# Second matrix of the MLP in seven block products instead of eight, with weight sums made by accumulating DMA

## The chip, the core and the metric

The kernel runs on one core of one Trainium2 chip. The metric is the device time of one execution in microseconds (us); the time before is the median of three runs. Four engines matter here: TensorE (PE in the profile; its weight loads are PEld), VectorE (DVE), ScalarE (ACT) and GpSimd (POOL). SyncE (SP) only issues DMAs.

## What is computed

One decoder layer on 512 tokens of width 1024, float32 throughout. A token mixer with three branches comes first (some 640 us of the time) and is not touched by the change. The part that is changed is the MLP behind it:

```python
h = rms_norm(x, norm_ffn_pre[l])
f = jnp.square(jax.nn.relu(h @ w_ff1[l])) @ w_ff2[l]
x = x + rms_norm(f, norm_ffn_post[l])
```

`w_ff1` is 1024 x 4096 and `w_ff2` is 4096 x 1024.

## The kernel before

Every float32 matrix product is made of three products in a rounded format: each operand is split into a high part (ScalarE copies it into the format, `copy_hi`) and a low part (VectorE subtracts the high part from the original, `lo`), and `products` (L936 to L938) issues high by high, high by low and low by high, in this order, into the same bank of PSUM. A matmul has a stationary operand of 128x128 and moves 512 columns.

Weights come as 176 "units" of 128x1024 (512 KB), in the order in which they are used. SyncE loads unit u into one of two raw slots (`raw`, L268) as soon as the low part of the unit before last in it is made. ScalarE copies it to `w_hi` (L375) when TensorE has finished unit u-4, because `w_hi` and `w_lo` are rings of four; VectorE makes `w_lo` (L603) behind it. TensorE waits for `w_lo_ready`, does the unit and counts up `unit_done`. So behind each finished unit ScalarE and VectorE prepare the unit four places on, and each engine works in the order of its program.

The hidden layer is worked in four quarters of 1024 channels. For each quarter there are eight "up" units (`up`, `channel_unit`: the weights are stationary, the 512 tokens move, eight steps of K, 24 matmuls, result in bank n of the eight banks) and eight "down" units (`token_unit`: 128 tokens by 128 hidden channels are stationary, 512 columns of weights move, four token chunks by two steps of K by three, 24 matmuls). The first three up units of a quarter are written ahead of the loop's end, which changes the program text but not the order.

Behind each up unit (`hidden_unit`) ScalarE makes relu from PSUM into one half of `duo` (L574) and its square into `a_hi` (L576), then splits the weights; VectorE splits the weights, squares in float32 (L885) and subtracts `a_hi` (L603). A down unit n below four waits for `hidden_lo` of the two tiles that it reads. After the fourth and the eighth down unit VectorE adds four banks into `by_token` in SBUF (L900). The last quarter is summed another way: its second half of weights is kept in `c_hi` and `c_lo`, and `resident_products` finishes one block of 128 tokens by 512 columns after another, so that the end of the kernel can overlap it.

GpSimd does little in this stage. It clears `by_token` (L367, 3.5 us, before the first quarter) and makes the inverse roots at the end.

Of the kernel before, what the change touches and what calls it, by code (L numbers as in the profile page):

```python
# [65 lines left out]
U_FF = U_OUT + KT  # L66
PER_QUARTER = 2 * KT
UNITS = U_FF + QUARTERS * PER_QUARTER

# [46 lines left out]
def build(nc, x_d, units_d, cols_d, rows_d, ws_d, bs_d, out_d):  # L116
    with ExitStack() as ctx:
        def sb(name, shape, dt=F32):
            return ctx.enter_context(nc.sbuf_tensor(name, shape, dt))

        def sem(name):
# [5 lines left out]
        w_lo = sb("w_lo", [P, RING, D], F32R)  # L127

        a_hi = sb("a_hi", [P, KT, SEQ], F32R)
        a_lo = sb("a_lo", [P, KT, SEQ], F32R)  # L130

        b_hi = sb("b_hi", [P, KT, SEQ], F32R)
        b_lo = sb("b_lo", [P, KT, SEQ], F32R)

# [22 lines left out]
        ws_lo = sb("ws_lo", [P, P], F32R)  # L157
        bs_row = sb("bs_row", [P, 2, P])
        duo = sb("duo", [P, 2, SEQ])
        th, h_copy = duo[:, 0, :], duo[:, 1, :]  # L160
        prod = sb("prod", [P, CONV_A - 1 + SEQ])
        y_a = sb("y_a", [P, SEQ])
# [14 lines left out]
        ps = ctx.enter_context(nc.psum_tensor("ps", [P, 8, 512], F32))  # L177


        raw_loaded = [sem(f"raw_loaded{n}") for n in range(RAW)]  # L180
        x_loaded = [sem(f"x_loaded{n}") for n in range(CH)]
# [65 lines left out]
        hidden_sq = sem("hidden_sq")  # L247
        hidden_lo = sem("hidden_lo")
        mlp_sum = sem("mlp_sum")
        out_weighted = sem("out_weighted")  # L250
# [14 lines left out]
        @block.sync  # L265
        def _(sp):
            def load(unit, slot):
                sp.dma_start(raw[:, slot, :], units_d[unit]).then_inc(raw_loaded[slot], 16)  # L268

            for c in range(CH):  # L270
                sp.dma_start(resid[:, c, :], x_d[c * P:(c + 1) * P, :]).then_inc(x_loaded[c], 16)
                if c < RAW:
                    load(c, c)
            sp.dma_start(cols[:, :, :], cols_d).then_inc(cols_loaded, 16)
            with sp.Fori(1, UNITS // RAW) as i:
                for slot in range(RAW):
                    sp.wait_ge(w_lo_ready, i * RAW + (slot - RAW + 1))
                    load(i * RAW + slot, slot)
            for c in range(CH):
# [8 lines left out]
        def _(pool):  # L288
# [77 lines left out]
            pool.wait_ge(turned, 4 * CH)  # L366
            nc.gpsimd.memset(wide[:, :], 0.0).then_inc(wide_cleared, 1)  # L367
            for c in range(CH):
                inverse_rms(3 * CH + c, 4 * CH + 2 * c, halves=True)
# [3 lines left out]
        def _(act):  # L373
# [3 lines left out]
            def split_hi(u, into=None, free=True):  # L377

                act.wait_ge(raw_loaded[u.raw], u.loads())
                if free and u.first >= RING:  # L380
                    act.wait_ge(unit_done, u.times(1, 1 - RING))
                copy_hi(w_hi[:, u.ring, :] if into is None else into,
                        raw[:, u.raw, :]).then_inc(w_hi_ready, 1)

            def after(u):
# [159 lines left out]
            def first_ff(units):  # L545
                for n in units:
                    act.wait_ge(unit_done, U_OUT + n + 1)
                    split_hi(Count(U_FF + n), free=False)

# [17 lines left out]

            def hidden_unit(u, n):

                after(u)  # L570
                if n.first % KT >= 2:
                    act.wait_ge(hidden_lo, n.times(1, -1))
                h = duo[:, n.first % 2, :]
                nc.scalar.activation(h, ps[:, n.first % KT, :], ACT.Relu).then_inc(hidden_relu, 1)  # L574
                act.wait_ge(hidden_relu, n.times(1, 1))
                nc.scalar.activation(a_hi[:, n.first % KT, :], h, ACT.Square).then_inc(hidden_hi, 1)  # L576
                split_hi(u.plus(RING))

            with act.Fori(0, QUARTERS - 1) as q:
                for n in range(KT):  # L580
                    hidden_unit(Count(U_FF + n, q, PER_QUARTER), Count(n, q, KT))
                for n in range(KT):
                    u = Count(U_FF + KT + n, q, PER_QUARTER)
                    after(u)
                    split_hi(u.plus(RING))
            for n in range(KT):
                hidden_unit(Count(U_FF + (QUARTERS - 1) * PER_QUARTER + n), Count((QUARTERS - 1) * KT + n))

            for n in range(CH):
                split_hi(Count(UNITS - CH + n), resident(c_hi, n), free=False)  # L590

            for c in range(CH):
                for half in range(2):
                    act.wait_ge(mlp_sum, ((QUARTERS - 1) * CH + c) * 2 + half + 1)
                    sum_squares(4 * CH + 2 * c + half, by_token[:, c, half * HALF:(half + 1) * HALF],
                                ps[:, 2 * c + half, :])
# [3 lines left out]
        def _(dve):  # L600
# [6 lines left out]
            def split_lo(u, into=None, hi=None):  # L607

                dve.wait_ge(w_hi_ready, u.times(1, 1))
                lo(w_lo[:, u.ring, :] if into is None else into, raw[:, u.raw, :],  # L610
                   w_hi[:, u.ring, :] if hi is None else hi).then_inc(w_lo_ready, 1)

            def after(u):
# [234 lines left out]
            for c in range(CH):  # L848
# [18 lines left out]
                if c == CH - 1:  # L867
                    split_lo(Count(U_FF + 2))
                dve.wait_ge(rstd_ready, CH + 2 * c + 2)
# [4 lines left out]
                for n in {CH - 2: (0, 1), CH - 1: (3,)}.get(c, ()):  # L874
                    split_lo(Count(U_FF + n))
            turned_lo(2 * CH - 1, CH - 1, b_hi, b_lo, 2 * (CH - 1))

            def hidden_unit(u, n):

                place = n.first % KT  # L880
                h = duo[:, n.first % 2, :]
                after(u)
                split_lo(u.plus(RING))
                dve.wait_ge(hidden_hi, n.times(1, 1))
                nc.vector.tensor_tensor(h, h, h, ALU.mult).then_inc(hidden_sq, 1)  # L885
                dve.wait_ge(hidden_sq, n.times(1, 1))
                lo(a_lo[:, place, :], h, a_hi[:, place, :]).then_inc(hidden_lo, 1)

            dve.wait_ge(wide_cleared, 1)
            with dve.Fori(0, QUARTERS - 1) as q:  # L890
                for n in range(KT):
                    hidden_unit(Count(U_FF + n, q, PER_QUARTER), Count(n, q, KT))
                for n in range(KT):
                    u = Count(U_FF + KT + n, q, PER_QUARTER)
                    after(u)
                    if n % CH == CH - 1:
                        half = n // CH
                        for c in range(CH):
                            y = by_token[:, c, half * HALF:(half + 1) * HALF]
                            nc.vector.tensor_tensor(y, y, ps[:, half * CH + c, :],  # L900
                                                    ALU.add).then_inc(mlp_sum, 1)
                    split_lo(u.plus(RING))
            for n in range(KT):
                hidden_unit(Count(U_FF + (QUARTERS - 1) * PER_QUARTER + n), Count((QUARTERS - 1) * KT + n))
            for n in range(CH):
                split_lo(Count(UNITS - CH + n), resident(c_lo, n), resident(c_hi, n))


            sums = (QUARTERS - 1) * 2 * CH
            dve.wait_ge(mlp_sum, sums)  # L910
# [22 lines left out]
        def _(pe):  # L933
# [173 lines left out]

            with pe.Fori(0, QUARTERS - 1) as q:
                for n in range(EARLY, KT):
                    up(Count(U_FF + n, q, PER_QUARTER), n)  # L1110
                for n in range(KT):
                    if n < CH:
                        pe.wait_ge(hidden_lo, Count(0, q, KT).times(1, 2 * n + 2))
                    token_unit(Count(U_FF + KT + n, q, PER_QUARTER), n % CH, n // CH, a_hi, a_lo)
                for n in range(EARLY):
                    up(Count(U_FF + PER_QUARTER + n, q, PER_QUARTER), n)
            for n in range(EARLY, KT):
                up(Count(U_FF + (QUARTERS - 1) * PER_QUARTER + n), n)
            before = (QUARTERS - 1) * KT
            resident_products(UNITS - KT, a_hi, a_lo, c_hi, c_lo,  # L1120
                              lambda piece: pe.wait_ge(hidden_lo, before + 2 * piece + 2),
                              lambda n, piece: None)
# [55 lines left out]
```

## Time and profile before

| | us |
|---|---|
| median of three runs (1006.65 to 1007.42) | 1007.12 |
| span of the profiled execution, first to last instruction | 1005.2 |
| what lies outside the span (median less span) | 1.9 |
| TensorE busy in the span | 986.9 |
| VectorE busy | 619.2 |
| ScalarE busy | 335.2 |
| GpSimd busy | 68.3 |

The median is that of timed runs; the profiled execution is known by its span. Busy times are read with care. A matmul's row gives the time from its start to its modelled end, and matmuls overlap, so what one matmul costs is the distance between two starts and not the length of a row. A timeline row gives the start in us from the span's start, the length in us, the engine, the line, the operation and the shapes, and in square brackets how long the engine sat idle before it and what released it. Rows with a count (x4) are several instructions merged. In the rows by stretch each engine's busy us stands with its number of instructions, then the granted clock of TensorE as a part of full speed, the mean busy share of the sixteen DMA engines (0.29 is 29%), and what they moved in GB/s.

### The profile page before, as it was taken

The page shows a single profiled execution, that of the slowest core. Times are in us where ns is not written, and L with a number is a line of the kernel's source. Part 1 is how long each engine was busy: PE and PEld are TensorE (multiplying, and loading weights), DVE is VectorE, ACT ScalarE, POOL GpSimd, SP SyncE. Part 2 cuts the span into 40 slices and gives each one's busy share as a digit, 9 for nine tenths or more (in the row PEclk, how much of TensorE's full clock was granted, in tenths as well). Part 3 has the DMA queues.
Part 4 walks back from the last instruction along what each step waited for, and adds up shares of the span by engine and source line. Part 5 has one row for each costly group of instructions (what it writes and reads, how often), then busy time and mean ns, then how long its engine had stood idle before and what let it go on. Part 6 is the DMA issues. An engine that isn't in the chain of part 4 may idle for free.

```text
span 1005.2 us, 12693 instructions
## 1 busy us (share of the span) xinstructions
PE 986.9 (98%) x4476; PEld 821.5 (82%) x4476; DVE 619.2 (62%) x765; ACT 335.2 (33%) x453; POOL 68.3 (7%) x83
## 2 busy tenths in 40 slices
PE   5999999999999999999999999999999999999997
PEld 4888888888888888888888888898888888888886
DVE  5348888888988988876674344844344334433545
ACT  5333332333233222224463232543224214313331
POOL 3000000000000011114000000210000000000001
PEclk9999999999999999999999999999999999999999
DMA  6323223233222222233245323132322323322222
GB/s 218 118 78 125 91 89 94 99 97 101 89 92 95 72 96 83 96 117 105 98 135 204 104 84 105 57 110 89 102 91 97 104 83 104 104 86 103 88 80 84
DMA packets 28861, 102.27 MB, mean 102 GB/s; under 512 B 3360, under 2 KB 3488, under 8 KB 28832
## 3 DMA queue, kind: packets, MB, share of 16 engines
q1 hardware_dynamic: 27216, 96.64, 28.6%
q10 hardware_dynamic: 1104, 4.19, 1.2%
q0 software_dynamic: 512, 1.05, 0.5%
q8 instruction: 18, 0.29, 0.1%
q14 instruction: 11, 0.09, 0.0%
HBM read 99.77 MB, written 2.10 MB: 101 GB/s over the span
## 4 chain that ended last, share of the span: by engine, by line
PE 98%; DMA 1%; DVE 1%; POOL 0%; ACT 0%; issue 0%; DVEq 0%; POOLq 0%; ACTq 0%
PE ps L936 31%; PE ps L937 31%; PE ps L938 31%; PE ps L1091 1%; PE ps L1090 1%; PE ps L1089 1%; PE ps L976 1%; DMA conf<-x_in 1%; PE ps L1039 0%; PE ps L1040 0%; PE ps L1038 0%; ACT ps L389 0%; DVE wide L628 0%; POOL rstd L310 0%; POOL meansq L306 0%; DVE a_lo L603 0%
## 5 line engine op out<-in xcount | busy, mean ns | idle before, releaser
L603 DVE TENSOR_TENSOR w_lo<-raw,w_hi 128x1024 fp32r<-128x1024 f32 x168 | 207.2, 1234 | 257.6 <-ACT w_hi L375 257.1
L375 ACT ACTIVATE w_hi<-raw 128x1024 fp32r<-128x1024 f32 x168 | 177.1, 1055 | 286.3 <-PE ps L938 217.6
L936 PE MATMUL ps<-a_hi,w_hi 128*128 128x512 f32 x576 | 225.4, 391 | 0.0
L937 PE MATMUL ps<-a_lo,w_hi 128*128 128x512 f32 x576 | 224.2, 389 | 0.0
L938 PE MATMUL ps<-a_hi,w_lo 128*128 128x512 f32 x576 | 224.1, 389 | 0.0
L674 DVE SCALAR_TENSOR_TENSOR conf<-glu,cols,conf (+1 forms) x240 | 186.8, 778 | 27.5 <-DVE conf L674 26.4
L936 PE MATMUL ps<-b_hi,w_hi 128*128 128x512 f32 x360 | 140.2, 390 | 0.0
L938 PE MATMUL ps<-b_hi,w_lo 128*128 128x512 f32 x360 | 140.1, 389 | 0.0
L937 PE MATMUL ps<-b_lo,w_hi 128*128 128x512 f32 x360 | 140.0, 389 | 0.0
L936 PEld LDWEIGHTS ps<-a_hi,w_hi 128*128 128x128 f32 x576 | 108.2, 188 | 22.7 <-DVE w_lo L603 0.2
L937 PEld LDWEIGHTS ps<-a_lo,w_hi 128*128 128x128 f32 x576 | 108.2, 188 | 22.6 <-issue 0.5
L938 PEld LDWEIGHTS ps<-a_hi,w_lo 128*128 128x128 f32 x576 | 108.1, 188 | 22.6
L936 PE MATMUL ps<-w_hi,a_hi 128*128 128x512 f32 x288 | 112.9, 392 | 1.5 <-DVE a_lo L603 1.4
L938 PE MATMUL ps<-w_hi,a_lo 128*128 128x512 f32 x288 | 112.5, 391 | 0.0
L937 PE MATMUL ps<-w_lo,a_hi 128*128 128x512 f32 x288 | 112.5, 391 | 0.0
L936 PEld LDWEIGHTS ps<-b_hi,w_hi 128*128 128x128 f32 x360 | 67.6, 188 | 14.3 <-DVE b_lo L604 0.3
L938 PEld LDWEIGHTS ps<-b_hi,w_lo 128*128 128x128 f32 x360 | 67.6, 188 | 14.1
L937 PEld LDWEIGHTS ps<-b_lo,w_hi 128*128 128x128 f32 x360 | 67.6, 188 | 13.9
L936 PEld LDWEIGHTS ps<-w_hi,a_hi 128*128 128x128 f32 x288 | 54.3, 189 | 13.3 <-DVE a_lo L603 2.2
L938 PEld LDWEIGHTS ps<-w_hi,a_lo 128*128 128x128 f32 x288 | 54.3, 189 | 11.5
L937 PEld LDWEIGHTS ps<-w_lo,a_hi 128*128 128x128 f32 x288 | 54.4, 189 | 11.1
L574 ACT ACTIVATE duo<-ps 128x512 f32<-128x512 f32 x32 | 19.1, 598 | 103.5 <-PE ps L938 96.4
(140 smaller groups left out, 891.7 us busy)
## 6 DMA issues: line engine op xcount, KB each, us to landing
raw<-units_in SPq DMA_DIRECT2D x176, 512.0 KB, 3.3
glu<-rows_in ACTq DMA_DIRECT2D x4, 512.0 KB, 10.9
conf<-x_in SPq DMA_DIRECT2D x4, 512.0 KB, 8.0
conf<-x_in ACTq DMA_DIRECT2D x1, 2048.0 KB, 9.2
y_out<-wide SPq DMA_DIRECT2D x8, 256.0 KB, 2.1
ws_raw<-ws_in POOLq DMA_DIRECT2D x8, 64.0 KB, 2.1
bs_row<-bs_in POOLq DMA_DIRECT2D x8, 64.0 KB, 3.1
cols<-cols_in SPq DMA_DIRECT2D x1, 156.0 KB, 9.2
```

The costliest lines, as they stand in the source:

```text
L375: return nc.scalar.activation(dst, src, ACT.Copy, scale=scale)
L574: nc.scalar.activation(h, ps[:, n.first % KT, :], ACT.Relu).then_inc(hidden_relu, 1)
L603: return nc.vector.tensor_tensor(dst, src, hi, ALU.subtract)
L674: nc.vector.scalar_tensor_tensor(out=conf[:, tile, :], in0=glu[:, tile, k:k + SEQ], scalar=cols[:, tile, COL_CONF + k:COL_CONF + k + 1], i ...
L936: nc.tensor.matmul(ps[:, bank, :], left_hi, right_hi, start=first, stop=False)
L937: nc.tensor.matmul(ps[:, bank, :], left_hi, right_lo, start=False, stop=False)
L938: return nc.tensor.matmul(ps[:, bank, :], left_lo, right_hi, start=False, stop=final)
L976: mm = nc.tensor.transpose(ps[:, banks + g, k * P:(k + 1) * P], by_token[:, c, at:at + P], ident[:, :])
L1089: nc.tensor.matmul(out, w_hi[:, u.ring, w], b_hi[:, k, tokens], start=k == 0, stop=False)
L1090: nc.tensor.matmul(out, w_hi[:, u.ring, w], b_lo[:, k, tokens], start=False, stop=False)
L1091: mm = nc.tensor.matmul(out, w_lo[:, u.ring, w], b_hi[:, k, tokens], start=False, stop=k == KT - 1)
```

## The change

The down products of the first three quarters are done in another way; the last quarter stays as it is. For one quarter the product is 512 tokens by 1024 hidden channels by 1024 columns. It is cut in halves along all three sides, and the eight half-size products are replaced by seven (Strassen's scheme, in a form with differences and sums). The steps are these:

- TensorE: the eight down units of 24 matmuls are replaced by 14 "pieces" (seven products in two halves of K each) of 12 matmuls, each with 128x128 stationary and 512 columns moving. The up units are the same, with the tiles of the hidden layer in the order 0, 4, 1, 5, 2, 6, 3, 7. The loop over quarters is written out.
- Left operands: seven blocks of 128x256 for each pair of hidden tiles instead of four. `hidden_pair`: ScalarE does relu of both tiles, each followed by the split of the weights four units on; one square of 128x1024 in place; a copy of two blocks into `set_hi`. VectorE makes five differences (`combo`, three instructions) and the low part of the two blocks. ScalarE copies the five differences into `set_hi`, and VectorE makes their low part. The square in float32 of VectorE (L885) goes.
- Right operands: five of the seven products need the sum or difference of two weight blocks. SyncE loads the first block; GpSimd issues a DMA with `accum_op=add` that adds the second block from memory to the one in the raw slot. For product 1 ScalarE first negates the block in the slot.
- Results: each product is added to or subtracted from one or two quarters of `by_token`, 24 instructions of 128x512 on VectorE for each quarter of the hidden layer instead of 8.
- Raw slots: eight instead of two, six of them laid over buffers that are no longer in use at this stage. `a_hi` and what follows it in SBUF are reused for `set_hi`, `set_lo` and two of the slots.

```diff
+PRODUCTS = {
+    3: (0, (0, 1), (1, 1), 2, ((0, 1, 1), (1, 1, 1))),
+    6: (2, (0, 0), (0, 1), 4, ((1, 1, 1),)),
...
+PIECES = ((3, 0), (6, 0), (3, 1), (6, 1), (4, 0), (2, 0), (4, 1), (2, 1),
+          (1, 0), (5, 0), (1, 1), (5, 1), (7, 0), (7, 1))
...
+NEGATED_AFTER = {0: 8, 2: 10}
...
+            for u in range(U_FF, UNITS):
+                slot = FF_SLOT[u]
+                if earlier_in_slot(u):
+                    sp.wait_ge(w_lo_ready, earlier_in_slot(u)[-1] + 1)
...
+                elif slot < 6:
+                    sp.wait_ge(unit_done, U_FF)
+                else:
+                    sp.wait_ge(mixed_in, 4 * CH)
+                sp.dma_start(slots[slot], units_d[source(u)]).then_inc(raw_loaded[slot], 16)
...
+                    if product == 1:
+                        negated += 1
+                        pool.wait_ge(raw_negated, negated)
+                    else:
+                        pool.wait_ge(raw_loaded[slot], ff_loads(u))
+                    pool.dma_start(slots[slot], units_d[source(u, second=True)],
+                                   accum_op=ALU.add).then_inc(raw_added[slot], 16)
...
+            def hidden_pair(q, p):
+
+                n = q * CH + p
+                for e in range(2):
+                    u = ff_unit(q, 2 * p + e)
+                    act.wait_ge(unit_done, u + 1)
+                    if n:
+                        act.wait_ge(set_lo_ready, 2 * n - 1)
+                    nc.scalar.activation(duo[:, e, :], ps[:, 2 * p + e, :], ACT.Relu).then_inc(hidden_relu, 1)
+                    ff_hi(u + RING)
+                act.wait_ge(hidden_relu, 2 * n + 2)
+                nc.scalar.activation(duo[:, :, :], duo[:, :, :], ACT.Square).then_inc(pair_squared, 1)
+                act.wait_ge(pair_squared, n + 1)
+                copy_hi(set_hi[:, 0:2, p, :], pair[:, 0:4:3, :]).then_inc(set_hi_ready, 1)
+                act.wait_ge(combo_ready, 3 * n + 3)
+                copy_hi(set_hi[:, 2:SETS, p, :], combo[:, :, :]).then_inc(set_hi_ready, 1)
...
+                for n in range(len(PIECES)):
+                    act.wait_ge(unit_done, piece_unit(q, n) + 1)
+                    ff_hi(piece_unit(q, n) + RING)
+                    if n in NEGATED_AFTER:
+                        u = piece_unit(q, NEGATED_AFTER[n])
+                        act.wait_ge(raw_loaded[FF_SLOT[u]], ff_loads(u))
+                        copy_hi(slots[FF_SLOT[u]], slots[FF_SLOT[u]], -1.0).then_inc(raw_negated, 1)
...
+                for e in range(2):
+                    u = ff_unit(q, 2 * p + e)
+                    dve.wait_ge(unit_done, u + 1)
+                    ff_lo(u + RING)
+                dve.wait_ge(pair_squared, n + 1)
...
+                nc.vector.tensor_tensor(combo[:, 0:2, :], pair[:, 1:4:2, :], pair[:, 0:4:2, :],
+                                        ALU.subtract).then_inc(combo_ready, 1)
+                nc.vector.tensor_tensor(combo[:, 2:4, :], pair[:, 2:4, :], pair[:, 0:2, :],
+                                        ALU.subtract).then_inc(combo_ready, 1)
+                nc.vector.tensor_tensor(combo[:, 4, :], pair[:, 0, :], pair[:, 3, :],
+                                        ALU.subtract).then_inc(combo_ready, 1)
+                dve.wait_ge(set_hi_ready, 2 * n + 1)
+                lo(set_lo[:, 0:2, p, :], pair[:, 0:4:3, :], set_hi[:, 0:2, p, :]).then_inc(set_lo_ready, 1)
+                dve.wait_ge(set_hi_ready, 2 * n + 2)
+                lo(set_lo[:, 2:SETS, p, :], combo[:, :, :], set_hi[:, 2:SETS, p, :]).then_inc(set_lo_ready, 1)
...
+                for n, (product, h) in enumerate(PIECES):
+                    dve.wait_ge(unit_done, piece_unit(q, n) + 1)
+                    ff_lo(piece_unit(q, n) + RING)
...
+                    for t in range(2):
+                        for m_half, n_half, sign in into:
+                            y = by_token[:, 2 * m_half + t, n_half * HALF:(n_half + 1) * HALF]
+                            nc.vector.tensor_tensor(y, y, ps[:, bank + t, :],
+                                                    ALU.add if sign > 0 else ALU.subtract).then_inc(mlp_sum, 1)
...
+            def piece(q, n):
...
+                ready(Count(u))
+                pe.wait_ge(set_lo_ready, 2 * (q * CH + 2 * h + 2))
+                if h == 0 and product in (3, 6, 4, 2):
+                    pe.wait_ge(hidden_relu, q * KT + bank + 2)
+                elif h == 0:
+                    pe.wait_ge(mlp_sum, sums_before(q, piece_done({1: 3, 5: 6, 7: 4}[product])))
+                for t in range(2):
+                    for k in range(2):
+                        at, w = slice(t * P, (t + 1) * P), slice(k * HALF, (k + 1) * HALF)
+                        mm = products(bank + t, set_hi[:, which, 2 * h + k, at], set_lo[:, which, 2 * h + k, at],
+                                      w_hi[:, u % RING, w], w_lo[:, u % RING, w],
+                                      (h, k) == (0, 0), (h, k) == (1, 1))
+                mm.then_inc(unit_done, 1)
```

An up unit of the next quarter also waits (`bank_summed`) until VectorE has emptied its bank.

## Rows read from the trace of the kernel before

**Rows 1.** The head and part 1 of the page.

```profile
span 1005.2 us, 12693 instructions
PE 986.9 (98%) x4476; PEld 821.5 (82%) x4476; DVE 619.2 (62%) x765; ACT 335.2 (33%) x453; POOL 68.3 (7%) x83
```

**Rows 2.** The page's part 4, the chain that ended last, by engine.

```profile
PE 98%; DMA 1%; DVE 1%; POOL 0%; ACT 0%; issue 0%; DVEq 0%; POOLq 0%; ACTq 0%
```

**Rows 3.** Busy time by stretch: us, engines, granted clock, DMA share, GB/s.

```profile
525.00:535.00 10.00, 10.00 (x46) 8.29 (x45) 4.34 (x5) 3.09 (x5) 0.00 (x0) 1.00 1.02 399
750.00:810.00 60.00, 60.00 (x266) 49.70 (x265) 25.29 (x30) 19.17 (x24) 0.00 (x0) 1.00 0.29 96
998.70:1005.20 6.50, 0.07 (x1) 0.00 (x0) 2.79 (x4) 0.72 (x2) 0.86 (x2) 0.82 0.21 81
```

**Rows 4.** Timeline (start, us, engine, line), TensorE, sixty matmuls of a down product.

```profile
789.62 0.39 PE L938 MATMUL ps<-w_hi,a_lo 128*128 128x512 f32 x1
...
803.00 0.39 PE L937 MATMUL ps<-w_lo,a_hi 128*128 128x512 f32 x1
```

**Rows 5.** Group by line and shape: busy us, mean ns, idle before.

```profile
L603 DVE TENSOR_TENSOR a_lo<-duo,a_hi 128x512 fp32r<-128x512 f32 x32 | 22.2, 692 | 1.1
```

**Rows 6.** Timeline, ScalarE, one hidden unit, and two weight copies back to back.

```profile
775.77 0.60 ACT L574 ACTIVATE duo<-ps 128x512 f32<-128x512 f32 x1 [3.23 <-PE ps L938]
776.40 0.63 ACT L576 ACTIVATE a_hi<-duo 128x512 fp32r<-128x512 f32 x1
776.94 1.04 ACT L375 ACTIVATE w_hi<-raw 128x1024 fp32r<-128x1024 f32 x1
...
956.46 1.04 ACT L375 ACTIVATE w_hi<-raw 128x1024 fp32r<-128x1024 f32 x1
957.40 1.04 ACT L375 ACTIVATE c_hi<-raw 128x1024 fp32r<-128x1024 f32 x1
```

**Rows 7.** Timeline, VectorE, one hidden unit, and the sums of one half.

```profile
778.01 1.22 DVE L603 TENSOR_TENSOR w_lo<-raw,w_hi 128x1024 fp32r<-128x1024 f32 x1 [2.89 <-ACT w_hi L375]
779.16 0.68 DVE L885 TENSOR_TENSOR duo<-duo 128x512 f32<-128x512 f32 x1
...
911.77 2.48 DVE L900 TENSOR_TENSOR wide<-wide,ps 128x512 f32<-128x512 f32 x4 [2.99 <-PE ps L938]
914.17 1.22 DVE L603 TENSOR_TENSOR w_lo<-raw,w_hi 128x1024 fp32r<-128x1024 f32 x1
```

**Rows 8.** Timeline, start of the kernel: TensorE resumes after a wait.

```profile
12.56 0.69 DVE L603 TENSOR_TENSOR a_lo<-ps,a_hi 128x512 fp32r<-128x512 f32 x1 [0.16 <-ACT a_hi L375]
...
13.30 0.29 PEld L936 LDWEIGHTS ps<-w_hi,a_hi 128*128 128x128 f32 x1 [1.81 <-DVE a_lo L603]
13.30 0.80 PE L936 MATMUL ps<-w_hi,a_hi 128*128 128x512 f32 x1 [1.41 <-DVE a_lo L603]
```

**Rows 9.** Timeline, TensorE, spacing early in the kernel and somewhat later.

```profile
13.89 0.63 PE L937 MATMUL ps<-w_lo,a_hi 128*128 128x512 f32 x1
...
14.32 0.63 PE L938 MATMUL ps<-w_hi,a_lo 128*128 128x512 f32 x1
...
19.16 0.40 PE L937 MATMUL ps<-w_lo,a_hi 128*128 128x512 f32 x1
19.39 0.39 PE L938 MATMUL ps<-w_hi,a_lo 128*128 128x512 f32 x1
```

**Rows 10.** The page's parts 3 and 6: DMA queues; issues with KB and us to landing.

```profile
q1 hardware_dynamic: 27216, 96.64, 28.6%
q0 software_dynamic: 512, 1.05, 0.5%
...
raw<-units_in SPq DMA_DIRECT2D x176, 512.0 KB, 3.3
ws_raw<-ws_in POOLq DMA_DIRECT2D x8, 64.0 KB, 2.1
```

**Rows 11.** Groups by line: what an issue costs GpSimd.

```profile
L318 POOL DMA_DIRECT2D ws_raw<-ws_in x8 | 4.7, 587 | 174.8 <-DVE y_s L757 174.8
```

More of the change, by code:

```diff
@@ L177, in build @@
         ps = ctx.enter_context(nc.psum_tensor("ps", [P, 8, 512], F32))
[L180 removed]
+        set_hi = over("set_hi", [P, SETS, CH, SEQ // 2], "a_hi", dt=F32R)
+        set_lo = over("set_lo", [P, SETS, CH, SEQ // 2], "a_hi", SETS * 2 * SEQ, dt=F32R)
+        raw_c = over("raw_c", [P, 2, D], "a_hi", SETS * 4 * SEQ)
+        raw_v = over("raw_v", [P, 2, D], "v_hi")
+        combo = over("combo", [P, SETS - 2, SEQ // 2], "y_a")
+        pair = duo[:, :, :].rearrange("p j (h t) -> p (j h) t", h=2)
+        slots = [raw[:, 0, :], raw[:, 1, :], raw_v[:, 0, :], raw_v[:, 1, :],
+                 raw_c[:, 0, :], raw_c[:, 1, :], row[0], row[1]]
+        raw_loaded = [sem(f"raw_loaded{n}") for n in range(SLOTS)]
+        raw_added = [sem(f"raw_added{n}") for n in range(SLOTS)]
+        raw_negated = sem("raw_negated")
         x_loaded = [sem(f"x_loaded{n}") for n in range(CH)]
@@ L383, in split_hi, with ff_hi @@
                         raw[:, u.raw, :]).then_inc(w_hi_ready, 1)
+            def ff_hi(u, into=None, free=True):
+                slot = FF_SLOT[u]
+                if has_second(u):
+                    act.wait_ge(raw_added[slot], seconds(u))
+                else:
+                    act.wait_ge(raw_loaded[slot], ff_loads(u))
+                if free:
+                    act.wait_ge(unit_done, u + 1 - RING)
+                copy_hi(w_hi[:, u % RING, :] if into is None else into, slots[slot]).then_inc(w_hi_ready, 1)
             def after(u):
@@ L874, in _ @@
                 for n in {CH - 2: (0, 1), CH - 1: (3,)}.get(c, ()):
-                    split_lo(Count(U_FF + n))
+                    ff_lo(U_FF + n)
             turned_lo(2 * CH - 1, CH - 1, b_hi, b_lo, 2 * (CH - 1))
[L878 to L884, printed above, removed]
-                nc.vector.tensor_tensor(h, h, h, ALU.mult).then_inc(hidden_sq, 1)
-                dve.wait_ge(hidden_sq, n.times(1, 1))
-                lo(a_lo[:, place, :], h, a_hi[:, place, :]).then_inc(hidden_lo, 1)
@@ L889, in _ @@
[L889 to L902, printed above, removed]
@@ L1117, in _, with bank_summed @@
-            for n in range(EARLY, KT):
-                up(Count(U_FF + (QUARTERS - 1) * PER_QUARTER + n), n)
-            before = (QUARTERS - 1) * KT
+            def bank_summed(q, n):
+                for product in {0: (2,), 2: (1,), 4: (5,), 6: (7,)}.get(n, ()):
+                    pe.wait_ge(mlp_sum, sums_before(q, piece_done(product)))
+            def piece(q, n):
+                product, h = PIECES[n]
+                which, _, _, bank, _ = PRODUCTS[product]
+                u = piece_unit(q, n)
+                ready(Count(u))
[11 more added lines that the diff above has]
+                mm.then_inc(unit_done, 1)
@@ L1120, in _ @@
+            for q in range(STRASSEN):
+                for n in range(EARLY if q == 0 else 0, KT):
+                    if q:
+                        bank_summed(q - 1, n)
+                    up(Count(ff_unit(q, n)), n)
+                for n in range(len(PIECES)):
+                    piece(q, n)
+            for n in range(KT):
+                bank_summed(STRASSEN - 1, n)
+                up(Count(U_LAST + n), n)
             resident_products(UNITS - KT, a_hi, a_lo, c_hi, c_lo,
-                              lambda piece: pe.wait_ge(hidden_lo, before + 2 * piece + 2),
+                              lambda piece: pe.wait_ge(hidden_lo, 2 * piece + 2),
```

148 lines of the change are left out of this document (107 added, 41 removed), and 5 rows, old and new, of the table PRODUCTS.

## Prediction

> **What bounds the kernel now.** I read the head of the page first, then the chain that ended last, then the stretches, then single rows. TensorE is busy for 986.9 of 1005.2 us [rows 1], and the chain is 98% TensorE [rows 2]. Busy time alone can deceive, since matmuls overlap, so the spacing decides: sixty matmuls in a row start between 789.62 and 803.00, 59 distances in 13.38 us, 0.2268 us each, over two unit boundaries and without a gap [rows 4]. One unit of 24 matmuls is 5.44 us, as the ScalarE rows also say: they come back every 5.44 us. In the MLP the clock is full, the DMA engines are 29% busy, VectorE works 25 of 60 us and ScalarE 19 [rows 3]. So in this stage only two things move the time: fewer matmuls, and gaps in TensorE's stream.
>
> **What the change removes.** Down products of one quarter: 8 x 24 = 192 matmuls become 14 x 12 = 168, all with 512 moving columns. Three quarters: 72 fewer, 72 x 0.2268 = 16.3 us. Nothing hides under it: it is the bounding engine.
>
> **What it adds ahead of the first late pieces.** This is the one place where I find a new wait. Before, the last hidden tiles of a quarter were needed only by the fourth down unit, 3 x 5.44 us later. Now the third piece (product 3, second half of K) waits for all of pair 3, and TensorE has only two pieces, 24 matmuls, 5.44 us, to do in between. The chain behind the quarter's eighth up unit, from the start of its relu (0):
>
> ScalarE. Relu 0.60 long; the next independent instruction can start 0.09 before a row's end (776.40 + 0.63 against 776.94), so the weight split starts at 0.51 and ends at 1.55. Two 1024-wide instructions follow at 0.94 [rows 6], so the square of 128x1024, priced like that split, runs 1.45 to 2.49. A dependent instruction starts 0.03 after the end (776.37 to 776.40): copy of two blocks, 512 wide, 2.52 to 3.15.
>
> VectorE. It starts 0.03 after ScalarE ends (777.98 to 778.01) and next starts 1.15 later [rows 7]: its weight split runs 1.58 to 2.81. Then the differences, at the 0.69 of a 512-wide subtraction [rows 5], 0.60 apart as the four sums are (2.40 us, [rows 7]): 2.73, 3.33, and the 256-wide one from 3.93. Its length by the slope between 512 and 1024 columns (1.22 less 0.69 for 512) is 0.42, so it ends at 4.35. The two blocks' low part goes 4.28 to 4.97.
>
> Then ScalarE copies five differences, 1280 wide: 1.04 plus half of the step from 512 to 1024 (1.04 less 0.63), 1.25, from 4.38 to 5.63. VectorE takes their low part, 1.22 plus 0.27, 1.49, from 5.66 to 7.15. TensorE resumes 0.05 after such a release (13.25 to 13.30, [rows 8]), and perhaps after one weight load of 0.2 more: 7.20 to 7.40.
>
> TensorE is free at 5.47 (the relu starts 0.20 after the last matmul's start, so the next starts at 0.03, and 24 x 0.2268 = 5.44). The gap is 1.7 to 1.9 us; I take 1.9, as a first matmul after a wait is also long [rows 8]. Three times: 5.7 us. Its lower end would be 3 x 1.3 if the shorter instructions come out cheaper, the upper 3 x 2.8 if the strided operands cost 0.2 for each of five steps on the chain; nothing in the rows shows strides.
>
> **What it adds elsewhere, and what covers it.** VectorE in the piece phase: a split of 1.15 for each piece and 24 sums at 0.60, so 14 x 1.15 + 14.4 = 30.5 us in 14 x 2.72 = 38.1. Followed piece by piece from 7.15, VectorE is latest where products 4 and 2 have handed it four sums each: the split for the thirteenth piece (product 7, first half) ends near 30.5, and TensorE wants it at 34.6. The cover is the ring of four, 4 us at the worst spot. If sums cost a quarter more (0.75), the 8 since its last idle moment add 1.2 us, which is still inside. Over a quarter VectorE has some 54 us of 83, ScalarE some 37.
>
> Up units that wait for their bank: the tightest is the third, whose bank product 1 leaves; its sums are made near 36, and the unit starts near 51. Free.
>
> The negation (two copies of 0.94 for each quarter on ScalarE) is queued behind the split for the fifth piece and ahead of that for the sixth; the sixth is needed 8 us later. Free.
>
> In the first quarter the new loads wait for `unit_done` and `mixed_in`, both over before 650 us, and are wanted from 661 on. Free. The longer list of waits on TensorE's queue is free so far as the gapless boundaries of [rows 4] go.
>
> **The DMAs, the unknown.** For each quarter there are 22 plain loads of 512 KB and 10 accumulates of 512 KB. A plain one costs the sixteen engines 0.29 x 60 / 11 = 1.6 us (one load in 5.44 us, [rows 3]). No row shows an accumulate. Its lower bound is a plain one, 1.6. GpSimd's own queue took 0.5% of the span, 5.0 us, for 1.05 MB, so 2.5 us for 512 KB [rows 10]; if the read of the slot doubles this, 5.0 is the upper bound. I take 3.2, twice a plain one, as it moves each byte of the slot in and out. Sum: 22 x 1.6 + 10 x 3.2 = 67 us in a quarter of 83.5 (51 and 85 at the bounds). The engines have run at full share, 399 GB/s, beside an undisturbed TensorE: 46 matmuls in 10 us [rows 3]. Throughput is then covered except at the upper bound.
>
> As to latency, most accumulates have over 20 us, as there are eight slots. The tightest is the first half of product 1: it waits for the negation, done near 7.6; its split is due at 15.6 and TensorE starves only if it lands after about 21, 13.8 us later. A plain load lands after 3.3, GpSimd's small ones after 2.1 [rows 10], and an issue keeps GpSimd 0.6 us [rows 11]. Even 8 us would do. GpSimd has nothing else queued behind these waits until the end of the kernel.
>
> The Trainium skill (Collectives: The Full Stack, "The bandwidth ceiling") says that an add in the DMA engines costs two source reads, which halves throughput. No row here can show it; by it an accumulate is the 3.2 that I took from bytes, and the sum stays. It also warns (SBUF — State Buffer, "Who interferes with whom") that DMAs issued by GpSimd starve while VectorE runs in its two-port modes; it lists `tensor_tensor` as having none, and nearly all of VectorE's work here is that, so by it no issue is held for longer than one instruction.
>
> **The sum.** Span 1005.2 - 16.3 + 5.7 = 994.6; the timed median lies 1.9 above the span, so 996.5 us.
>
> **Rivals.**
> A. Forecast, 996.5 (994 to 1000 with the ends of the gap), 66%.
> B. The gap isn't there, or is under 1 us for each quarter: 1007.1 - 16.3 + up to 3 = 991 to 994. For it: the square's and the copies' prices are all from other shapes. Against: the chain would have to be 1.9 shorter in seven steps. 7%.
> C. The gap is right, and smaller ones come beside it, from VectorE's queue in the piece phase or from a late accumulate: 1 to 3 us more for each quarter, 1000 to 1005. For it: VectorE is at 80% there. 11%.
> D. TensorE's clock falls after each gap. At the kernel's start, after 10 us of idling, matmuls stood 0.43 us apart, the 1.2 GHz level, and 0.23 by 19.2 us [rows 9]: 9 us at half rate. If each of the three gaps brought that, 3 x 4.5 = 13.5 on top: 1010, slower than before. Against: in that very stretch there was a gap of 1.4 us [rows 8], and the clock rose all the same; at the kernel's end it stood at 0.82 with TensorE idle for 6.4 us [rows 3]. 4%. The Trainium skill (TensorE: Matmul & The Clock Gate, "What's actually happening") has the clock fall after an idle stretch; these rows agree only for gaps far longer than mine.
> E. Accumulates dearer than the bound. A quarter takes 35 + 10 A us of DMA; with A above 4.9 it outlasts TensorE's 83.5, above 5.2 the 87.0 of before. At 6.4, four times a plain one, it is 99: 12 us more than before for each of some two and a half quarters that the slots don't cover, with the last quarter's start: about 1035 at worst, 1015 to 1025 likelier. For it: nothing in the trace shows the operation. Against: 5.0 is already both doublings at once. 12%.
>
> **How the numbers follow.** Chances: faster by over 0.2% (below 1005.1; 0.2% is about what a measurement of this kernel can tell from no change) has A, B and C, 0.82 after a little of C is given away; slower (above 1009.1) has D and E but for their mild ends, 0.13; within 0.2%, 0.05. The range must leave out no more than 2 in 10: 992 to 1004 leaves out half of B, a little of C, and D and E.
>
> **What would show it.** Right: matmuls of the three quarters still 0.2268 apart, a piece 2.72 us; 72 fewer 512-wide ones; three idle stretches of about 1.9 us before the third piece of a quarter, released by VectorE's low part of the five differences; ScalarE never waiting on an accumulate. Wrong: TensorE idle put down to a weight split behind a DMA (C, E), DMA share near 1 in the piece phase (E), spacing of 0.43 after a gap (D), no idle at the third piece (B). The likeliest single error is the 1280-wide pair of steps, 2.7 us of the chain, priced by slopes.

## The result, and the profile after

The changed kernel takes 1001.83 us (median of four runs, 1001.18 to 1002.63) against 1007.1 us for the kernel before beside it: a ratio of 0.9948, 95% interval 0.9936 to 0.9961. That is 5.3 us faster, in the range of 992 to 1004, but half of the 10.6 us that was forecast as likeliest.

The page of the changed kernel: span, busy times, two of the DMA queues (packets, MB, share of sixteen engines' span).

```profile
span 1000.9 us, 12382 instructions
PE 976.5 (98%) x4404; PEld 811.6 (81%) x4404; DVE 680.0 (68%) x843; ACT 377.1 (38%) x489; POOL 94.2 (9%) x113
...
q1 hardware_dynamic: 29808, 106.08, 31.3%
q0 software_dynamic: 4832, 16.78, 9.0%
```

This answers [rows 1] and [rows 10]. TensorE has 72 matmuls fewer (4404 after 4476), and its busy time fell by 10.4 us, not by 16.3. So TensorE itself became slower somewhere. Who waited for what on TensorE in the stretch of the MLP (us in total, times, longest):

```profile
PE ps L1117 <- DVE set_lo L758: 6.0, 3, 2.0
```

Three waits of 2.0 us, behind VectorE's low parts of the five differences, as forecast. The chain that was worked out step by step can be laid beside its rows. ScalarE and VectorE behind the eighth up unit of the first quarter (columns as in [rows 6] and [rows 7]):

```profile
694.41 0.60 ACT L713 ACTIVATE duo<-ps 128x512 f32<-128x512 f32 x1 [3.72 <-PE ps L1119]
694.91 1.05 ACT L501 ACTIVATE w_hi<-raw_v 128x1024 fp32r<-128x1024 f32 x1
695.86 1.05 ACT L716 ACTIVATE duo<-duo 128x1024 f32<-128x1024 f32 x1
696.94 0.64 ACT L501 ACTIVATE set_hi<-duo 128x512 fp32r<-128x512 f32 x1
698.86 1.28 ACT L501 ACTIVATE set_hi<-combo 128x1280 fp32r<-128x1280 f32 x1 [1.29 <-DVE combo L1053]
```

```profile
696.06 1.23 DVE L758 TENSOR_TENSOR w_lo<-raw_v,w_hi 128x1024 fp32r<-128x1024 f32 x1 [4.04 <-ACT w_hi L501]
697.21 0.69 DVE L1049 TENSOR_TENSOR combo<-duo 128x512 f32<-128x512 f32 x1
697.81 0.68 DVE L1051 TENSOR_TENSOR combo<-duo 128x512 f32<-128x512 f32 x1
698.41 0.42 DVE L1053 TENSOR_TENSOR combo<-duo 128x256 f32<-128x256 f32 x1
698.75 0.68 DVE L758 TENSOR_TENSOR set_lo<-duo,set_hi 128x512 fp32r<-128x512 f32 x1
700.17 1.49 DVE L758 TENSOR_TENSOR set_lo<-combo,set_hi 128x1280 fp32r<-128x1280 f32 x1 [0.74 <-ACT set_hi L501]
```

From relu to the end of the last row 7.25 us pass (694.41 to 701.66), where 7.15 were forecast. Then TensorE, before and behind the gap:

```profile
699.43 0.39 PE L1119 MATMUL ps<-w_hi,set_lo 128*128 128x512 f32 x1
701.81 0.47 PE L1117 MATMUL ps<-w_hi,set_hi 128*128 128x512 f32 x1 [1.99 <-DVE set_lo L758]
702.12 0.40 PE L1118 MATMUL ps<-w_lo,set_hi 128*128 128x512 f32 x1
...
703.09 0.63 PE L1119 MATMUL ps<-w_hi,set_lo 128*128 128x512 f32 x1
703.52 0.63 PE L1117 MATMUL ps<-w_hi,set_hi 128*128 128x512 f32 x1
...
706.08 0.54 PE L1117 MATMUL ps<-w_hi,set_hi 128*128 128x512 f32 x1
706.45 0.39 PE L1118 MATMUL ps<-w_lo,set_hi 128*128 128x512 f32 x1
706.68 0.39 PE L1119 MATMUL ps<-w_hi,set_lo 128*128 128x512 f32 x1
```

The next matmul would have started at 699.66 and starts at 701.81, 2.15 us later. The reader should look at the distances behind it: 0.23 us at first, 0.43 us from 703.09 to 706.08, and 0.23 again from 706.45. The granted clock says the same:

```profile
702.00:703.00 1.00, 1.00 (x5) 0.82 (x5) 0.80 (x1) 0.98 (x2) 0.68 (x1) 0.99 0.00 0
703.00:706.00 3.00, 3.00 (x8) 2.31 (x8) 1.22 (x1) 0.00 (x0) 0.18 (x1) 0.50 0.69 128
706.00:707.00 1.00, 1.00 (x5) 0.79 (x4) 0.00 (x0) 0.60 (x1) 0.00 (x0) 0.81 0.99 258
```

At 0.50 of full speed, the 1.2 GHz level, the matmuls stand 0.43 us apart instead of 0.227. From 702.81 to 706.45 there are nine distances, 3.64 us, where nine at 0.227 would be 2.04: 1.6 us lost. The other two quarters look alike (gaps of 2.15 us, long distances from 788.3 to 791.7 and from 873.5 to 877.2), and by the granted clock each of the three low stretches lasts 3.4 us. Gap, clock and the first matmul's extra 0.1 us come to 3.84 us for a quarter. The balance is 16.3 - 3 x 3.84 = 4.8 us gained; the medians give 5.3, the spans 4.3.

### The profile page after: what moved, and what is told of

Same layout as the page of the kernel before. It is cut to its first block, busy times and chain, and to the rows that moved or that the text cites. A ratio compares the mean times of both kernels' runs of the same rounds, so it can differ in the third digit from the quotient of the medians.

```text
span 1000.9 us, 12382 instructions
## 1 busy us (share of the span) xinstructions
PE 976.5 (98%) x4404; PEld 811.6 (81%) x4404; DVE 680.0 (68%) x843; ACT 377.1 (38%) x489; POOL 94.2 (9%) x113
## 4 chain that ended last, share of the span: by engine, by line
PE 96%; DVE 1%; ACT 1%; issue 1%; DMA 1%; POOL 0%; DVEq 0%; POOLq 0%; ACTq 0%
PE ps L1117 31%; PE ps L1118 30%; PE ps L1119 30%; PE ps L1157 1%; PE ps L1272 1%; PE ps L1271 1%; PE ps L1270 1%; DMA conf<-x_in 1%; DVE set_lo L758 0%; ACT set_hi L501 0%; PE ps L1220 0%; PE ps L1221 0%; PE ps L1219 0%; ACT w_hi L501 0%; DVE combo L1049 0%
## 5 line engine op out<-in xcount | busy, mean ns | idle before, releaser
L758 DVE TENSOR_TENSOR w_lo<-raw,w_hi 128x1024 fp32r<-128x1024 f32 x130 | 160.6, 1237 | 128.3 <-ACT w_hi L501 127.9
L501 ACT ACTIVATE w_hi<-raw 128x1024 fp32r<-128x1024 f32 x130 | 137.2, 1056 | 197.6 <-PE ps L1119 129.0
L1117 PEld LDWEIGHTS ps<-a_hi,w_hi 128*128 128x128 f32 x576 | 108.2, 188 | 22.6 <-DVE w_lo L758 0.2
L1119 PEld LDWEIGHTS ps<-a_hi,w_lo 128*128 128x128 f32 x576 | 108.1, 188 | 22.6
L1118 PEld LDWEIGHTS ps<-a_lo,w_hi 128*128 128x128 f32 x576 | 108.2, 188 | 22.6 <-issue 0.5
L1117 PE MATMUL ps<-w_hi,set_hi 128*128 128x512 f32 x168 | 67.4, 401 | 6.0 <-DVE set_lo L758 6.0
L1119 PE MATMUL ps<-w_hi,set_lo 128*128 128x512 f32 x168 | 67.4, 401 | 0.0
L1118 PE MATMUL ps<-w_lo,set_hi 128*128 128x512 f32 x168 | 67.4, 401 | 0.0
L1075 DVE TENSOR_TENSOR wide<-wide,ps 128x512 f32<-128x512 f32 x72 | 44.7, 678 | 0.0
L1117 PEld LDWEIGHTS ps<-w_hi,set_hi 128*128 128x128 f32 x168 | 32.8, 195 | 14.2 <-issue 7.2
L758 DVE TENSOR_TENSOR w_lo<-raw_v,w_hi 128x1024 fp32r<-128x1024 f32 x20 | 24.4, 1222 | 28.1 <-ACT w_hi L501 28.1
L1117 PE MATMUL ps<-w_hi,a_hi 128*128 128x512 f32 x96 | 38.2, 398 | 1.8 <-DVE a_lo L758 1.8
```

The source lines that it names most:

```text
L501: return nc.scalar.activation(dst, src, ACT.Copy, scale=scale)
L758: return nc.vector.tensor_tensor(dst, src, hi, ALU.subtract)
L1075: nc.vector.tensor_tensor(y, y, ps[:, bank + t, :], ALU.add if sign > 0 else ALU.subtract).then_inc(mlp_sum, 1)
L1117: nc.tensor.matmul(ps[:, bank, :], left_hi, right_hi, start=first, stop=False)
L1118: nc.tensor.matmul(ps[:, bank, :], left_hi, right_lo, start=False, stop=False)
L1119: return nc.tensor.matmul(ps[:, bank, :], left_lo, right_hi, start=False, stop=final)
```

## The experiments

The theory to be tested: the loss is the gap and, behind it, TensorE's clock, which falls because of the gap. The main rival: the slow matmuls come from what is new beside TensorE, the accumulating DMAs or VectorE's sums. All runs below stand beside a kernel before of 1007.2 us.

**Another order of the pieces.**

```diff
-PIECES = ((3, 0), (6, 0), (3, 1), (6, 1), (4, 0), (2, 0), (4, 1), (2, 1),
+PIECES = ((3, 0), (6, 0), (4, 0), (2, 0), (3, 1), (6, 1), (4, 1), (2, 1),
```

> The changed kernel with its pieces in another order: the first halves of products 3, 6, 4 and 2 stand before any second half, so TensorE has four pieces (10.9 us) to do while the last pair of hidden tiles is prepared (7.4 us). Theory 1 (a gap of 2.15 us ahead of the third piece, and then matmuls 0.43 us apart for about 3.6 us, 1.6 us lost, because the clock falls after the gap; 3.8 us for each of three quarters): both go, 1007.1 - 16.3 = 991, up to 993 if late accumulates leave small gaps. Theory 2 (the gap costs 2.15 us, and the slow matmuls come from the accumulating DMAs or VectorE's sums beside TensorE): the gap goes and the slow stretch stays, 1001.8 - 6.5 = 995.4.

Measured: 990.85 us (990.65 to 991.27), ratio 0.9838, interval 0.9825 to 0.9851. The whole 16.35 us are there (1007.2 - 990.85), with the same DMAs, sums and splits. No gap, no slow stretch: the busy time of TensorE fell by 15.3 us against [rows 1].

```profile
span 989.5 us, 12382 instructions
PE 971.6 (98%) x4404; PEld 809.3 (82%) x4404; DVE 679.7 (69%) x843; ACT 376.4 (38%) x489; POOL 94.2 (10%) x113
```

**The gap filled with work that is thrown away.**

```diff
                 for n in range(len(PIECES)):
+                    if n == 2:
+                        for _ in range(9):
+                            nc.tensor.matmul(ps[:, 0, :], b_hi[:, 0, 0:P], b_hi[:, 0, :], start=True, stop=True)
                     piece(q, n)
```

> The changed kernel with nine extra matmuls of 512 columns (2.04 us of work that is thrown away) ahead of the third piece of each quarter, so that TensorE works through the wait and stands idle for at most 0.2 us. Theory 1 (clock falls after the idle stretch): no stretch of 0.43 us spacing, 1001.8 - 3 x 1.6 = 997.0. Theory 2 (slow matmuls come from DMAs or VectorE beside them): the time of the changed kernel, 1001.8, and the slow stretch stays.

Measured: 997.84 us (997.72 to 998.02), 4.0 us below the changed kernel. TensorE around the third piece:

```profile
699.66 0.39 PE L1119 MATMUL ps<-w_hi,set_lo 128*128 128x512 f32 x1
699.89 2.20 PE L1321 MATMUL ps<-b_hi 128*128 128x512 f32 x9
702.04 0.47 PE L1117 MATMUL ps<-w_hi,set_hi 128*128 128x512 f32 x1
702.35 0.40 PE L1118 MATMUL ps<-w_lo,set_hi 128*128 128x512 f32 x1
...
703.49 0.39 PE L1117 MATMUL ps<-w_hi,set_hi 128*128 128x512 f32 x1
```

The third piece starts 2.15 us after the fillers begin, at the very place where it started before, since it still waits for the same chain. But the distances stay 0.23 us. So the kernel with all of its gap's delay and none of the slow stretches is 997.8, and the clock is worth the rest: 1001.8 - 997.8 = 4.0 us, between two and three falls at 1.6 us. (997.0 was expected, from 4.8 us for three falls in every execution.)

**Hardly any accumulate traffic.** Only 64 of 1024 columns are added; most of the weight sums are left out.

```diff
-                    pool.dma_start(slots[slot], units_d[source(u, second=True)],
+                    pool.dma_start(slots[slot][:, 0:64], units_d[source(u, second=True)][:, 0:64],
```

> The changed kernel, but each accumulating DMA adds only 64 of the 1024 columns, so most of the sums of weight blocks are left out; every wait stays. Theory 1: the accumulates cost nothing, 1001.8 within 0.5. Theory 2: with a sixteenth of their traffic the slow stretch after the gap goes, 997.0.

Measured: 999.51 us (999.23 to 1002.33), which is neither number. The trace explains it: the gaps are the same 2.15 us in all three quarters, but the clock fell behind one of them only. Behind the first:

```profile
699.55 0.39 PE L1119 MATMUL ps<-w_hi,set_lo 128*128 128x512 f32 x1
701.93 0.47 PE L1117 MATMUL ps<-w_hi,set_hi 128*128 128x512 f32 x1 [1.99 <-DVE set_lo L758]
...
703.39 0.40 PE L1117 MATMUL ps<-w_hi,set_hi 128*128 128x512 f32 x1
703.63 0.39 PE L1118 MATMUL ps<-w_lo,set_hi 128*128 128x512 f32 x1
```

One fall on top of 997.8 gives 999.4; the run of 1002.33 had a mean granted clock of 0.993, as the slowest runs of the changed kernel, the others 0.996. So a gap of 2.15 us doesn't always bring a fall. Nor does the fall always come at the same place: behind the second gap the clock was down with the first matmul (785.81), behind the gaps of the changed kernel only about 1 us after it. Whether the smaller traffic made falls rarer, or chance did, this run doesn't settle; but with most of that traffic gone the gap is the same, and the full fall can still be had.

**The kernel before with a gap.** One wait moved in the loop of the first three quarters.

```diff
-                        pe.wait_ge(hidden_lo, Count(0, q, KT).times(1, 2 * n + 2))
+                        pe.wait_ge(hidden_lo, Count(0, q, KT).times(1, KT))
```

> The kernel before with one wait moved: in the first three quarters the first down unit waits for all eight hidden tiles. No products of blocks, no accumulates, only a gap for TensorE, from the last matmul of the up units (781.0) to the last low part (786.0) by the rows of before: 5.0 us for each quarter. Theory 1: the gap also lets the clock fall, 1.6 us or more each: 1007.1 + 3 x (5.0 + 1.6) = 1026.9 or above. Theory 2: 1007.1 + 15.0 = 1022.1, spacing 0.227 all through.

Measured: 1029.79 us (1028.62 to 1030.35), 22.6 us above the kernel before.

```profile
694.03 0.39 PE L938 MATMUL ps<-b_hi,w_lo 128*128 128x512 f32 x1
699.38 0.79 PE L936 MATMUL ps<-w_hi,a_hi 128*128 128x512 f32 x1 [4.96 <-DVE a_lo L603]
699.96 0.63 PE L937 MATMUL ps<-w_lo,a_hi 128*128 128x512 f32 x1
700.39 0.63 PE L938 MATMUL ps<-w_hi,a_lo 128*128 128x512 f32 x1
```

Without any part of the change the gap (5.12 us beyond the usual distance) is followed at once by distances of 0.43 us, those of [rows 9]. Gaps account for 15.4 us, the clock and the first matmuls for the other 7.2, some 2.4 for each gap. By the granted clock the falls came 2.2, 3.6 and 4.3 us into the three idle stretches, so the time since the last matmul doesn't fix the moment of a fall. The rival falls: neither accumulates nor sums are needed for the clock to fall.

**The changed kernel again.**

> The changed kernel as it is, on this chip, beside the next three. Its runs so far lie between 1001.2 and 1002.6. If each of the three gaps lets the clock fall or not by chance, the runs stand in steps of about 1.6 us, between 997.8 (no fall) and 1002.6 (three), and the mean granted clock of a run (0.998 to 0.993) tells how many it had. If the falls are no chance, all runs are alike, near 1001.8.

Measured: 1001.13 us; the five runs are 1002.06, 1002.02, 1001.13, 1001.05 and 1000.89, with mean granted clocks of 0.993, 0.993, 0.995, 0.996 and 0.996. There are steps, but only the upper ones: at 1.6 us for a fall on top of 997.8 the times say two or three falls in each run, never none. The mean granted clock puts the runs in about the same order but doesn't count falls, since it also takes in a fall behind the kernel's last matmul, which costs nothing and whose low stretch differs from run to run (4.4 us in the first profile of this kernel, 5.3 in this one). The profiled run had three gaps of 2.15 us and a fall behind each; for the others the number is read from their times.

**Less idle time: four extra matmuls, then two.** The diff is that of the nine, with `range(4)` and `range(2)`.

> The changed kernel with four extra matmuls (0.9 us) ahead of the third piece, so that 1.2 us of the 2.15 us stay idle. The third piece can't start sooner, so 997.8 (the time with nine extra matmuls) is the floor. Theory 1a (the length of the idle stretch decides whether the clock falls): 998, no slow stretch. Theory 1b (any idle stretch will do): 1001.8 as before, each with a slow stretch.

Measured: 997.54 us (997.54 to 997.76). The clock stayed up behind all gaps, so an idle stretch of 1.2 us (the profile: 1.09) does no harm beyond its length. Then the length between:

> The changed kernel with two extra matmuls (0.45 us) ahead of the third piece: 1.7 us stay idle, between the 1.1 to 1.2 us that left the clock alone and the 2.15 us that let it fall two or three times out of three. If the fall depends on the length of the idle stretch: 997.6 (never) to 1001.8 (mostly), and the mean granted clock of a run says which; somewhere between, 998 to 1000, is likeliest. If the third piece still starts when the chain ends, no fall means 997.6.

Measured: 997.56 us (997.27 to 997.84), no fall either, where a mixture was called likeliest. Columns as above, the idle time before an instruction in brackets:

```profile
699.15 0.39 PE L1119 MATMUL ps<-w_hi,set_lo 128*128 128x512 f32 x1
699.38 0.61 PE L1321 MATMUL ps<-b_hi 128*128 128x512 f32 x2
701.53 0.47 PE L1117 MATMUL ps<-w_hi,set_hi 128*128 128x512 f32 x1 [1.54 <-DVE set_lo L758]
701.85 0.39 PE L1118 MATMUL ps<-w_lo,set_hi 128*128 128x512 f32 x1
```

Idle for 1.54 us by the profile: no fall in three gaps of the profiled run, and none to be seen in the times of four. Idle for 1.99: two or three falls of three in the changed kernel. The difference is two thrown-away matmuls, 0.45 us for each quarter, which are worth 3.6 to 4.3 us. The changed kernel was not run again beside this one, but the kernel with four raw slots was (the last experiment): its clock fell behind each of its six idle stretches of 2.0 to 2.8 us and behind none of its six of 0.4 to 0.9 us.

**The chain made shorter.** For the last pair ScalarE squares and copies two blocks before it splits weights, and VectorE splits them last.

```diff
-                    ff_hi(u + RING)
+                    if (p, e) != (CH - 1, 1):
+                        ff_hi(u + RING)
...
                 copy_hi(set_hi[:, 0:2, p, :], pair[:, 0:4:3, :]).then_inc(set_hi_ready, 1)
+                if p == CH - 1:
+                    ff_hi(ff_unit(q, KT - 1) + RING)
...
-                    dve.wait_ge(unit_done, u + 1)
-                    ff_lo(u + RING)
+                    if (p, e) != (CH - 1, 1):
+                        dve.wait_ge(unit_done, u + 1)
+                        ff_lo(u + RING)
...
                 lo(set_lo[:, 2:SETS, p, :], combo[:, :, :], set_hi[:, 2:SETS, p, :]).then_inc(set_lo_ready, 1)
+                if p == CH - 1:
+                    dve.wait_ge(unit_done, ff_unit(q, KT - 1) + 1)
+                    ff_lo(ff_unit(q, KT - 1) + RING)
```

> The changed kernel, in which for the last pair of hidden tiles ScalarE squares and copies before it splits the weights four units on, and VectorE splits them last. By the rows of the changed kernel the chain from relu to TensorE is 6.3 us instead of 7.4 us, and the gap 1.05 instead of 2.15 us: 1007.2 - 16.35 + 3 x 1.15 = 994.3 if the clock stays up, 999.1 if it falls each time. Were the gap set by anything but this chain (a load, an accumulate, a bank), it would stay: 1001.8.

Measured: 994.43 us (993.81 to 994.68), with gaps of 1.09 us in the trace (1.05 expected) and no fall. The chain was made 1.1 us shorter and the gap followed by as much, so it is the chain that sets the gap.

**Three first halves ahead instead of two.**

```diff
-PIECES = ((3, 0), (6, 0), (3, 1), (6, 1), (4, 0), (2, 0), (4, 1), (2, 1),
+PIECES = ((3, 0), (6, 0), (4, 0), (3, 1), (6, 1), (2, 0), (4, 1), (2, 1),
```

> The changed kernel with three pieces instead of two ahead of the first that needs the last pair (first halves of 3, 6 and 4): 8.2 us of work against a chain of 7.4 us. Theory 1 (the chain alone decides): no gap, 991.0. If anything later than 7.4 us also holds these pieces up (the first splits of weights behind the chain, end near 8.7): a gap of 0.5 us, 992.5 or above.

Measured: 991.01 us (990.82 to 991.07). One piece more, 2.72 us of work, covers a gap of 2.15 us.

**What the raw slots are worth.** The reordered kernel with fewer slots in turn.

```diff
-FF_SLOT = {U_FF + n: n % SLOTS for n in range(U_LAST - U_FF)}
+FF_SLOT = {U_FF + n: n % 6 for n in range(U_LAST - U_FF)}
```

> The reordered kernel (four first halves ahead), with six raw slots in turn instead of eight. A slot is busy for load (4.8), accumulate (8.2) and both splits (2.3), and waits between, 15.5 to 16 us by the medians of that kernel's profile; six slots come back every 6 x 2.72 = 16.3 us. Theory (the DMAs are covered by the number of slots): 991 to 993. If there is plenty of cover: 990.9.

Measured: 991.12 us (990.94 to 991.32): six are enough. With `n % 4`:

> The reordered kernel with four raw slots in turn. A slot comes back every 4 x 2.72 = 10.9 us, but needs some 16 us when its unit has an accumulate: pieces come every 4 us where all have one, and TensorE waits on splits behind DMAs. 14 pieces x 1.2 us less the 4 us that the ring holds: 5 to 12 us for each of three quarters, 1006 to 1027, slower than before at the upper end. If the slots buy nothing: 990.9.

Measured: 1023.17 us (1021.81 to 1023.88), ratio 1.0154, slower than before. Waits of that kernel in the stretch of the MLP (engine, buffer and line, releaser: us in total, times, longest), and the first pieces' stretch beside a later one (columns as in [rows 3]):

```profile
PEld ps L1117 <- DVE w_lo L758: 24.6, 12, 3.3
ACT w_hi L501 <- DMA raw<-units_in: 22.5, 7, 7.8
ACT raw_v L501 <- DMA raw_v<-units_in: 20.2, 3, 7.1
PE ps L1117 <- DVE w_lo L758: 19.5, 12, 2.8
ACT raw L501 <- DMA raw<-units_in: 19.0, 3, 7.1
```

```profile
700.00:720.00 20.00, 15.51 (x60) 11.97 (x58) 6.20 (x6) 7.51 (x9) 2.58 (x3) 0.91 0.57 143
740.00:780.00 40.00, 40.00 (x177) 33.11 (x178) 26.42 (x34) 18.94 (x23) 3.46 (x4) 1.00 0.69 175
```

TensorE waits for weight splits four times in each quarter, and the clock falls with it (0.91 in the first stretch). What the splits wait for is of two kinds. The two longest waits of each quarter, 15.5 of the 19.5 us, end with a split that stood in ScalarE's queue behind a negation (the rows `raw` and `raw_v`), and the negation waited for a plain load into a slot that had only just come free: the first one idle from 701.24 to 706.76. The two shorter ones, 4.0 us in all, end with a split that itself waited for a DMA into its slot. The DMA engines are busy for only 57% in the first stretch, so it is waiting for slots and landings that counts there, not the bandwidth. How much of the 32 us above the reordered kernel would stay if the negation stood later in ScalarE's queue, no run shows.

## Why the prediction was right or wrong

**Fewer matmuls, 16.3 us: right.** The reordered kernel shows it bare, 16.35 us.

**The gap, 1.9 us for each quarter with ends of 1.3 and 2.8: right in place and releaser, short by 0.25.** The instructions were priced well, the 1280-wide ones among them (1.28 and 1.49 against 1.25 and 1.49), and TensorE resumed 7.40 us after the relu's start, the upper end that was given. What was wrong is when it is free: 5.25 us after the relu's start (694.41 to 699.66), not 5.47. "The relu starts 0.20 after the last matmul's start" took a row of the next unit (775.57) for the last one of the unit; in the changed kernel the relu of 694.41 starts 0.42 after the unit's last matmul (693.99). Counted by the right matmul the forecast would have been 2.15.

**TensorE's clock behind the gap: this is the step that failed.** The sum put it at nothing, and it measured 4.0 us (1001.8 less the 997.8 of the kernel with nine fillers); the other 1.3 us of the miss (997.8 less 996.5) are left for the gap, of which its length explains 3 x 0.25. It stood among the rivals as D, with 4%, and was dismissed for two reasons. One was the gap of 1.4 us early in the kernel, behind which the clock rose all the same. But the matmuls right behind that gap stand 0.43 us apart [rows 9], and no row ahead of it shows full speed: such a gap can show that a rise isn't prevented, and says nothing on whether a clock at full speed stays up. (The granted clock reads 1.00 at that place, 13 to 15 us, so only the distances show the level there.) For a clock at full speed the later runs have it: no fall behind three idle stretches of 1.54 us in a profiled execution, seven falls behind nine of 1.99.

The other reason was the end of the kernel, 6.4 us idle at a mean of 0.82, read as a clock that needs a far longer idle stretch. By finer stretches that fall came at 1002.8, 4.1 us after the last matmul. That is one case of several: in the kernel before with a gap a fall came 2.2 us after the last matmul, and in the changed kernel 2.9 to 3.2 us after, when TensorE had been idle for 1.99 us and had worked again for about 1 us.

The price was wrong the other way: 4.5 us for each fall, from the length of the slow stretch at the kernel's start, where the fall costs 1.6. With 4.5 the rival came out slower than before and so looked like an outsider; with 1.6 it would have given 996.5 + 3 x 1.6 = 1001.3, within 0.6 of what came. The Trainium skill (TensorE: Matmul & The Clock Gate, "What's actually happening") ties the level to recent activity, and the traces agree: 0.50 behind a gap of 2.15 us, 1.00 where fillers ran in it.

**The DMAs: covered, as forecast.** GpSimd's queue has 9.0% of sixteen engines' span, 8.5% without the small loads of [rows 10]: 0.085 x 1000.9 / 30 = 2.8 us for an accumulate, where 3.2 was taken and 1.6 to 5.0 were the bounds. It lands later than a plain load, as these issues of the changed kernel show (KB, median us to landing):

```profile
raw<-units_in SPq DMA_DIRECT2D x134, 512.0 KB, 3.3
...
raw<-units_in POOLq DMA_DIRECT2D x9, 512.0 KB, 7.8
...
raw_c<-units_in POOLq DMA_DIRECT2D x7, 512.0 KB, 9.3
```

Some 8 to 9 us where the prediction said that "even 8 us would do", and nobody waits. (In the reordered kernel, where TensorE comes sooner, ScalarE's splits did wait for DMAs, 19 us in all by its groups, and the ring of four hid that.) Narrow accumulates changed nothing that the number of clock falls doesn't explain. That the cover is the slots, and ends between six and four, only the last two runs showed. With four the negation, rightly called free with eight, is what holds up the splits most. Rival E (throughput) did not come, and by 22 x 1.6 + 10 x 2.8 = 63 us in a quarter of some 85 it couldn't.

**VectorE's cover in the piece phase: right.** It has the same 72 sums in the reordered kernel, four products closer together, and that kernel has no gap. Rival B (no gap) is out. C gave nearly the right time, 1000 to 1005, but for causes that aren't there: TensorE has no further gaps, and ScalarE's weight splits waited for TensorE alone, never for a DMA, as this group shows for one pair of slots (busy us, mean ns, idle before and what ended it):

```profile
L501 ACT ACTIVATE w_hi<-raw_c 128x1024 fp32r<-128x1024 f32 x16 | 16.9, 1056 | 14.2 <-PE ps L1119 14.2
```

## What to carry to other kernels

When TensorE's work between a producer and its consumer is halved, count again what stood between them: here the order of four pieces was worth 11 us, twice what the rest of the change had left. A gap on a bounding TensorE can have two prices, its length and the clock behind it; if a gap of some 2 us can't be moved, shorten it, or run a few matmuls that nobody needs in it. And price a rival with the rows of the thing itself, since a price that is too high hides a likely one.

## What the runs showed of the hardware

- TensorE's clock fell to 0.50 for 3.4 us behind idle stretches of 1.99 us: three times of three in two profiled runs, where it began 0.9 to 1.2 us after work had resumed, and once of three in the run with narrow accumulates, where it began with the first matmul. In the kernel with four slots it fell behind all six idle stretches of 2.0 to 2.8 us. Behind 1.54 us and less it never fell in the profiled runs. Behind 4.96 us it was down from the first matmul on, having fallen 2.2 to 4.3 us into the idle stretch. What decides between a fall and none at 1.99 us, and when it comes, is open.
- A fall costs 1.6 us behind such a gap (nine distances of 0.40 on average for 0.227), 2.4 us behind 5 us with the long first matmul.
- An accumulating DMA of 512 KB from memory into SBUF takes 2.8 us of the sixteen engines' time and lands after 7.6 to 9.4 us in company, 3.3 to 4.6 for plain loads.
